# Dividing the filling matmuls of an attention unit around its transposes (two trunk layers on one core)

## What is computed

```python
mod = cond @ p['w_mod'] + p['b_mod']                       # six sections per layer
...
s = jnp.einsum('bhqcd,bhkcd->cbhqk', qi, k32) * scale      # two score maps, c = 0 and 1
pr = jax.nn.softmax(s, axis=-1)
o = jnp.einsum('bhqk,bhkd->bhqd', pr[0] - lam * pr[1], v32)
o = rms_norm(o, p['subln_g']) * (1.0 - lam_init)
y = jnp.concatenate([y_a, y_b, o], axis=-1) @ p['w_out']
```

## Time and profile before

| | us |
|---|---|
| median of three executions | 1689.54 |
| lowest, highest of the three | 1686.64, 1689.78 |
| the profiled execution | 1686.68 |
| its span, first to last instruction of the program | 1684.8 |

### The profile page before, as it was taken

One profiled execution on the slowest core, in us unless ns is written; L12 is line 12 of the kernel. 1 busy time (PEld: TensorE's weight loads), 2 busy tenths in 40 slices (PEclk: granted clock), 3 DMA queues, 4 the chain that ended last, 5 costly groups with the idle time before them and its releaser, 6 DMA issues.

```text
span 1684.8 us, 23039 instructions
## 1 busy us (share of the span) xinstructions
PE 1559.6 (93%) x7996; PEld 802.8 (48%) x7996; DVE 866.6 (51%) x2815; ACT 362.0 (21%) x792; POOL 469.1 (28%) x437
## 2 busy tenths in 40 slices
PE   6999899899998999999979997998999989999996
PEld 2886355444444444444447853563444444444443
DVE  3789653644444444434266987455444344444432
ACT  2521443111111111111153224440111111111111
POOL 0350010233333233333114301004333333233320
PEclk9999999999999999999989999999999999999998
DMA  9422915799999999999732248039999999999993
GB/s 399 155 102 105 380 84 200 288 410 413 413 413 416 413 412 414 412 415 412 299 131 100 101 161 357 1 110 398 388 412 414 413 415 412 413 413 413 415 413 164
DMA packets 80853, 530.62 MB, mean 315 GB/s; under 512 B 13968, under 2 KB 17308, under 8 KB 25184
## 3 DMA queue, kind: packets, MB, share of 16 engines
q1 hardware_dynamic: 67680, 503.90, 73.7%
q0 software_dynamic: 13056, 25.22, 4.0%
HBM read 533.76 MB, written 5.77 MB: 320 GB/s over the span
## 4 chain that ended last, share of the span: by engine, by line
PE 65%; DMA 25%; DVE 5%; ACT 2%; issue 2%; SPq 1%; POOL 0%; DVEq 0%; ACTq 0%
PE PSB L978 24%; DMA RING<-in_exp_w_up 13%; DMA WB<-in_exp_w_up 9%; PE PSB L991 8%; PE PSB L885 4%; PE PSB L1025 3%; PE PSB L1026 3%; PE PSB L970 2%; DMA RING<-in_wmod 2%; PE PSB L702 2%; PE PSB L921 1%; PE PSB L948 1%; PE PSB L931 1%; PE PSB L922 1%; PE PSB L947 1%
## 5 line engine op out<-in xcount | busy, mean ns | idle before, releaser
L978 PE MATMUL PSB<-RING,EX 128*32 128x512 f32 (+2 forms) x1408 | 373.3, 606 | 27.3 <-DMA RING<-in_exp_w_up 14.1
L978 PE MATMUL PSB<-WB,EX 128*32 128x512 f32 (+2 forms) x1344 | 371.5, 598 | 22.9 <-DMA WB<-in_exp_w_up 13.0
L576 POOL DMA_INDIRECT XG<-h_rows,IDX x272 | 279.8, 1029 | 146.5 <-issue 72.8
L585 POOL TENSOR_SCALAR SCAT<-CST,LSTT 128x384 fp32r<-128x384 f32 x68 | 85.6, 1259 | 560.8 <-DVE IDX L1863 519.1
L991 PE MATMUL PSB<-RING,AT 128*32 128x512 f32 (+2 forms) x752 | 210.8, 597 | 0.0
L978 PEld LDWEIGHTS PSB<-RING,EX 128*32 128x32 f32 (+2 forms) x1408 | 115.9, 126 | 182.0 <-issue 182.0
L978 PEld LDWEIGHTS PSB<-WB,EX 128*32 128x32 f32 (+2 forms) x1344 | 114.4, 127 | 177.4 <-issue 177.4
L1939 DVE TENSOR_TENSOR YL<-PSB,YH 128x512 fp32r<-128x512 f32 x136 | 94.1, 692 | 188.9 <-ACT YH L1431 188.9
L991 PE MATMUL PSB<-WB,AT 128*32 128x512 f32 (+2 forms) x672 | 189.1, 597 | 0.0
L1855 DVE COPY LCOL<-PSB 128x6 f32<-128x6 f32 x68 | 11.2, 165 | 338.8 <-PE PSB L1009 293.9
L1025 PE MATMUL PSB<-YH,SCAT 128*128 128x512 f32 x408 | 171.7, 421 | 2.8 <-DVE YL L1939 2.8
(11 more groups left out here) (299 smaller groups left out, 2005.8 us busy)
## 6 DMA issues: line engine op xcount, KB each, us to landing
RING<-in_exp_w_gate SPq DMA_DIRECT2D x64, 1024.0 KB, 14.5
RING<-in_exp_w_up SPq DMA_DIRECT2D x64, 1024.0 KB, 18.0
WB<-in_exp_w_gate SPq DMA_DIRECT2D x64, 1024.0 KB, 14.7
WB<-in_exp_w_up SPq DMA_DIRECT2D x64, 1024.0 KB, 19.0
RING<-in_exp_w_down SPq DMA_DIRECT2D x64, 1024.0 KB, 18.4
WB<-in_exp_w_down SPq DMA_DIRECT2D x64, 1024.0 KB, 19.0
RING<-in_wmod SPq DMA_DIRECT2D x16, 2048.0 KB, 11.8
KSYS<-in_wmod SPq DMA_DIRECT2D x8, 2048.0 KB, 10.8
```

The costliest lines, as they stand in the source:

```text
L576: pool.indirect_dma_start(XG[:, s % 2, g * 256:(g + 1) * 256], None, h_quarters, bass.IndirectOffsetOnAxis(ap=IDX[:, s, g:g + 1], axis=0), ...
L585: nc.gpsimd.tensor_scalar(SCAT[:, s % 2, :], cst("iota"), LSTT[:, s:s + 1], None, ALU.is_equal).then_inc(p_scat, 1)
L978: mm = nc.tensor.matmul(PS[6][s0:s0 + w, :].rearrange("p (w f) -> p w f", w=2), e(k, s0, w), rawgu[n % NBUF][:, k], start=(k == 0), stop=( ...
```

## The change

The filling work of an iteration is divided. The first half (for a chunk the four matmuls of `hf` 1, with the wait for the chunk's load; for a piece its first f) is issued between the scores and the transposes, ahead of the wait for DVE's difference. The second half (`hf` 0, with the release of the slot; the second f) stays where all of it was, behind the transposes. `conv_root` and `mod_columns` keep their places. No instruction is added or taken away. The core of the diff:

```diff
-            def mod_chunk(j):
+            def mod_chunk(j, halves=(1, 0)):
 ...
+                if 1 in halves:
+                    if j == 0:
+                        pe.wait_ge(d_cond, 3)
+                    elif sec == first and part == 0:
+                        pe.wait_ge(a_mod, 2 * g)
+                    pe.wait_ge(chunk_in[a], 16 * n)
                 w = chunk[a].rearrange("p (c n) -> p c n", c=4)
-                for hf in (1, 0):
+                for hf in halves:
 ...
-                mm.then_inc(mod_used, 1)
+                if 0 in halves:
+                    mm.then_inc(mod_used, 1)
 ...
-            def w_out_piece(l, p):
-
-                if p == 0:
+            def w_out_piece(l, p, n):
+
+                if p + n == 0:
                     pe.wait_ge(a_OT, NUN * l + 4)
                     pe.wait_ge(d_ln, K_LN * (l + 1))
-                w_out(l, 0, p // 4, 2 * (p % 4), 2 * (p % 4) + 2)
+                w_out(l, 0, p // 4, 2 * (p % 4) + n, 2 * (p % 4) + n + 1)
 ...
                     if i == 1:
                         conv_var(l)
+                    j, g = fill(l, i)
+                    if j is not None:
+                        mod_chunk(j, (1,))
+                    for p in pieces(l, i):
+                        w_out_piece(l, p, 0)
                     if 1 <= i <= NUN:
                         u = i - 1
 ...
                     if i == 3:
                         conv_root(l)
-                    j, g = fill(l, i)
                     if g is not None:
                         pe.wait_ge(d_ln, K_LN * l + 7)
                         mod_columns(g)
                     if j is not None:
-                        mod_chunk(j)
+                        mod_chunk(j, (0,))
                     for p in pieces(l, i):
-                        w_out_piece(l, p)
+                        w_out_piece(l, p, 1)
 ...
                 for p in range(7, 8):
-                    w_out_piece(l, p)
+                    w_out_piece(l, p, 0)
+                    w_out_piece(l, p, 1)
```

## The result

The changed kernel takes 1694.89 us (median of 20, 1690.69 to 1699.72), the kernel before 1687.94 us beside it. The ratio is 1.0038 with a 95% interval of 1.0029 to 1.0047: about 6.4 us slower (4.9 to 7.9). The forecast was 1690.7, a sum of +2.6; the time lies at the upper end of the range (1694.8), 0.1 us beyond it, and the likeliest case, within 0.2%, did not come. Three single executions far from the rest (8413.93 us of the kernel before, 2297.60 and 4452.58 us in the experiments) are left out of the ratios.

What follows compares the result with a forecast made beforehand. DVE, full from iteration 6 to attention times values of iteration 8, was taken to bound both attention loops. 0.9 + 1.7 + 0 = +2.6 us on a middle of 1688.1 gave 1690.7 us, range 1687.0 to 1694.8.

Steps and rivals of the forecast that it cites:

- the likeliest case: Whole kernel: a time within about 0.2% (3.4 us) of the kernel before, chance 0.69.
- Gaps while DVE is full: TensorE's long gaps in iterations 7 and 8: filling them shortens nothing, as DVE is busy without a pause.
- Rival (a): Iterations 5 to 7 and the short later waits: filled gaps pay, 4.1 us faster at most, 1684.0 us; chance 0.06.
- Iteration 5: Transposes start behind the load's landing and a half chunk: 0.8 to 1.0 us later, first layer; +1.7 us, second.
- the prediction's 197.5: First layer: time in us when PD of unit 4 ends, 1.0 later because of iteration 3.
- Iteration 3: One transpose and `conv_root` come after the load lands: 1.0 us (0.2 to 2.0) towards PD of unit 4; hidden in second layer.
- Iterations 9 to 12: Late exponentials against filled short waits: taken as 0 per layer, ends +0.6 and -0.64 us.
- (c): Iterations 9 to 11, both layers: exponentials late in every unit, 3.6 us more, 1694.3 us; chance 0.20.
- The clock: Granted clock of 0.50 after iterations 7 and 8, at 218.4 to 221.8 and 1048 to 1051: costs 3.2 us.
- rival b: A half in iteration 7's gap keeps the clock at 2.4 GHz: 3.2 us less, 1687.5 us; chance 0.12.

Runs made afterwards that it cites:

- e1: Changed kernel with the output projection's pieces whole behind the transposes again, only the modulation chunks divided; 1694.03 us, ratio 1.0044 to the kernel before.
- e4: Changed kernel with `mod_columns` of iteration 8 issued ahead of its transposes, in the wait for DVE; 1691.57 us, ratio 1.0020 to the kernel before.
- e11: Kernel before with only the chunks of iterations 3 and 5 divided, other chunks and pieces whole; 1690.46 us, ratio 1.0011.
- pieces alone: Changed kernel with the chunks whole behind the transposes again, only the output projection's pieces divided; 1686.89 us, ratio 0.9998 to the kernel before.

## Where the prediction was right and where not

*Gaps while DVE is full* were judged rightly: the waits for DVE fell by 1.7 us in the first loop and nothing came of it. Rival (a) is out.

*Iteration 5* was right: +1.10 us at the first maximum of iteration 6 for the 0.8 to 1.0 of the first layer, where PD, late by iteration 3, came last, as in the prediction's 197.5; +1.67 for 1.7 in the second with this half alone.

*Iteration 3*, taken at 1.0 us with ends of 0.2 and 2.0, was set somewhat low: about 1.6 us by the profiles of all kernels. In the profile of the change it is far more, from the start of the chunk to the scores of unit 4 1030.93 - 1024.66 = 6.27 us in the second loop, before 2.39: +3.9, as half a chunk, transpose, `conv_root` and the other half ran at half clock, and before nothing of it did. So PD of unit 4 came later than the load, the transposes of iteration 5 waited 0.35 us for it, and the second loop is 2.6 us late at this point and not 1.7. That is this one execution: in the profiles of the three other kernels with both halves (e1, e4, e11) the first maximum of iteration 6 in the second loop is 1.64 to 1.70 us later than before. Iteration 3 is hidden there, as forecast.

*Iterations 9 to 12* at 0 were right (pieces alone), ends and all, and (c), to which the prediction gave most of its chance of a slower kernel, was not how it got slower.

*The clock* is the step that failed. The prediction knew that it falls after iteration 8, priced 3.2 us for it, and asked only whether a half could keep it up (rival b). It did not ask what stands to be caught if the fall comes sooner: the transposes of iteration 8 and `mod_columns`, 1.85 us of work right ahead of where it fell, which was done just when DVE was and so had no room to get longer. The same price was to be had with the other sign. Its reason against (b), that iteration 8 keeps its gap, was right. In the first layer that gap even grew, from 0.94 to 2.61 us, and a fall that the prediction's rows don't hold is why: before, the chunk of iteration 7 ran at half clock as well (3.61 us from 208.11 on) and filled the gap of iteration 8, while DVE set the pace and nothing was lost. After the change the clock was up there, and down at the columns. The Trainium skill ("TensorE: Matmul & The Clock Gate", "Why this matters for your kernels") advises against long idle gaps between bursts of matmuls. The runs agree only in part: ahead of the columns a gap of 2.60 us came with the full clock (second layer of before) and one of 2.61 us with half of it (the change), so the gap by itself does not decide.

So +2.6 us were forecast for the order and are there (1.9 to 3.2), and the rest of the 6.4, 3 to 4.5 us that go with the clock, is what the sum lacked. That the time still came out at the end of the range is no merit of the mechanism: the range's upper end stood for rival (c).

## What to carry to other kernels

Work that is divided to fill the waits of an engine that doesn't set the pace moves the idle time to the next wait (here 2.5 us per loop ahead of the values). Where the trace shows a fall of the clock, price both signs: what it would give back if it went away, and what lies ahead of it, on the path or with no room beside it, and would be caught if it came sooner. And look at more than one execution before a stretch is sized: here the clock fell in other places from one to the next. Ahead of the scores' consumers put only work whose input has landed; a half behind a late load costs what runs on behind it (here 2.60 us at the transposes, where the trace of before had given 2.61).

## What the runs showed that was not expected

Eight matmuls of eight columns (`mod_columns`, sixteen records) took 1.85 us at a granted clock of 1.00 and 3.42 at 0.50, nearly the full factor of 2 for so small a step, though their weight loads fill most of that time (PEld 1.75 of 1.85 and 3.42 of 3.42 us). So the weight load gets longer with the lower clock as well, here from 192 ns to 333.

In the change the clock stayed at 0.50 for 10.24 us from 215.00 on, with TensorE busy 9.64 us of them; before it was 3.4 us from 218.4 on the earlier trace rows, behind another such fall at the chunk of iteration 7. A busy engine did not have it back at once:

```profile
215.00:225.24 10.24, 9.64 (x35) 7.10 (x36) 5.55 (x18) 2.47 (x9) 1.10 (x2) 0.50 0.38 163
```
